# Paged attention with gathers of eight-key rows, five sets of pages, and the next weights loaded at the end of the stage

## What is computed

```
def paged_attend(q_lat, q_pe, ckv_new, kpe_new, cache_ckv, cache_kpe, page_table, layer):
    ...
    def page_step(carry, pages):
        ck = cache_ckv[layer, pages]
        kp = cache_kpe[layer, pages]
        return online_update(carry, mla_scores(q_lat, q_pe, ck, kp), ck), None
    carry, _ = lax.scan(page_step, init, page_table.T)
```

## Time and profile before

| | us |
|---|---|
| median of 3 runs | 3132.86 |
| lowest, highest | 3125.3, 3133.38 |
| the profiled execution: span from first to last instruction | 3130.1 |
| PE busy in it | 2904.4 (93%) |
| DVE busy | 1737.1 (55%) |
| POOL busy | 1274.1 (41%) |
| ACT busy | 1076.9 (34%) |
| `stage_paged` in it, first to last matmul of the stage (lines 3158 to 3222) | 601.8 to 1039.5 |

### The profile page before, as it was taken

One profiled execution on the slowest core, in us unless ns is written; L12 is line 12 of the kernel. 1 busy time (PEld: TensorE's weight loads), 2 busy tenths in 40 slices (PEclk: granted clock), 3 DMA queues, 4 the chain that ended last, 5 costly groups with the idle time before them and its releaser, 6 DMA issues. The chain is left out here.

```text
span 3130.1 us, 60385 instructions
## 1 busy us (share of the span) xinstructions
PE 2904.4 (93%) x24873; PEld 2612.3 (83%) x24873; DVE 1737.1 (55%) x3025; ACT 1076.9 (34%) x2174; POOL 1274.1 (41%) x899
## 2 busy tenths in 40 slices
PE   6999899898899898999999998898898999999996
PEld 4888576566656798999999997887898999999996
DVE  5331245465555477666665237787477666664234
ACT  5411136421111464333331015575464333331012
POOL 2411157633333463444443114686553444443112
PEclk8999989898888999999999999999999999999999
DMA  9455300255554241232237322311331223246322
GB/s 318 163 201 182 103 22 1 89 177 178 189 183 163 78 132 56 98 112 93 103 116 276 110 102 86 87 30 30 85 119 63 96 100 112 85 139 252 140 81 79
DMA packets 241598, 377.90 MB, mean 121 GB/s; under 512 B 15531, under 2 KB 156204, under 8 KB 241061
## 3 DMA queue, kind: packets, MB, share of 16 engines
q1 hardware_dynamic: 200092, 253.95, 24.6%
q0 software_dynamic: 20992, 75.51, 7.2%
q10 hardware_dynamic: 20240, 44.57, 3.9%
HBM read 298.71 MB, written 73.28 MB: 119 GB/s over the span
## 5 line engine op out<-in xcount | busy, mean ns | idle before, releaser
L791 PE MATMUL ps<-HS,w_split 128*128 128x272 f32 x1920 | 272.2, 292 | 23.9 <-ACT sg L1048 10.4
L791 PEld LDWEIGHTS ps<-HS,w_split 128*128 128x128 f32 x1920 | 252.7, 190 | 29.8 <-ACT sg L1048 15.5
L807 PE MATMUL ps<-HS,w_ring 128*128 128x272 f32 x1920 | 273.0, 288 | 0.0
L807 PEld LDWEIGHTS ps<-HS,w_ring 128*128 128x128 f32 x1920 | 253.8, 189 | 0.0
L2312 PEld LDWEIGHTS ps<-HS_in,w_split 128*128 128x128 f32 x1728 | 222.7, 191 | 27.7 <-issue 16.4
L2312 PE MATMUL ps<-HS_in,w_split 128*128 128x272 f32 x1728 | 233.6, 294 | 9.2 <-DVE HS_in L2531 9.1
L1786 DVE TENSOR_TENSOR Y<-Y,ps 128x272 f32<-128x272 f32 x256 | 111.9, 437 | 224.9 <-PE ps L807 224.9
L1384 POOL TENSOR_TENSOR w_split<-w_raw,w_split 128x512 fp32r<-128x512 f32 x120 | 169.6, 1427 | 156.8 <-ACT w_split L1040 156.8
L762 PE MATMUL ps<-HS,w_ring 128*128 128x272 f32 x1344 | 179.8, 295 | 18.1 <-PEq L156 12.1
L762 PEld LDWEIGHTS ps<-HS,w_ring 128*128 128x128 f32 x1344 | 175.7, 193 | 20.5 <-POOLq L1433 12.3
L1384 POOL TENSOR_TENSOR w_ring<-w_raw,w_ring 128x512 fp32r<-128x512 f32 x40 | 61.5, 1538 | 270.1 <-ACT w_ring L1040 270.1
(11 more groups left out here) (496 smaller groups left out, 6695.9 us busy)
## 6 DMA issues: line engine op xcount, KB each, us to landing
hid_spill<-hid SPq DMA_DIRECT2D x40, 1088.0 KB, 7.4
w_mod_half<-w_mod_in SPq DMA_DIRECT2D x40, 1024.0 KB
HS<-hid_spill ACTq DMA_DIRECT2D x32, 1088.0 KB, 11.8
w_raw<-w_ffn_gate_in SPq DMA_DIRECT2D x44, 512.0 KB
w_raw<-w_ffn_up_in SPq DMA_DIRECT2D x44, 512.0 KB, 6.0
w_raw<-w_ffn_down_in SPq DMA_DIRECT2D x44, 512.0 KB
x_part<-x_spill SPq DMA_DIRECT2D x54, 272.0 KB, 2.9
x_spill<-Y SPq DMA_DIRECT2D x12, 1088.0 KB, 5.5
```

The costliest lines, as they stand in the source:

```text
L791: ins = pe.matmul(psum(U.banks(u)[b]), part_slot(j, a)[:, k, :], token_part(n, j, e)[:, k, :], start=(j < 3 and k == 0 and i == 0), stop=( ...
L807: ins = pe.matmul(down_bank(n), slots[DOWN_SLOT[t]][:, a, d * P:(d + 1) * P], hid_cols(k, t, q)[:, e, :], start=(t == lo and j == 0), stop ...
```

## The change

1. **Rows of eight keys.** The row table counts rows of 8 keys (`ROWK`, `NROWK = 8`), so a `cache_ckv` gather brings 8 KB per partition, 1 MB in all, and there are two for a period, one for each sequence, where there were four.
2. **Five sets of pages.** The buffers are five sets (`NSETS`) of one period each: `w_raw` with one old slot (`first.units[0]`), two sets in `q_all`, a new tile `pages_ckv1`, and `pages_ckv2`, which lies over slots 2 and 3 of the weight ring. DVE waits once for a period's whole set.
3. **When gathers are issued.** The gathers of period h wait for `scored` to count h-2, which is the end of `scores(h-3)`, and for `values(h-5)`. The `cache_kpe` gathers of an even h come after its two `cache_ckv` gathers, not before them. In `stage_attention` the early gathers bring set 0 and the two at its end bring set 1.
4. **The next weights come at the end.** SP loads the two `w_out_ab` tiles after `values(30)`, ACT splits them after `copy_p(31)` and ahead of the last copy into `Y`, and POOL after its last gather.

```diff
     def gather_pages(...)
-        i, j = g // NG, g % NG
-        blocks = c.cache_ckv[0].rearrange("n (h k) r -> (n h) (k r)", h=2 * NG)
-        pool.indirect_dma_start(out.rearrange("p a r -> p (a r)"), None, blocks,
-                                bass.IndirectOffsetOnAxis(c.ckv_rows[:, 2 * i + e, j:j + 1], 0)).then_inc(done, 16)
+        i, n = h // NUNIT, NROWK // NUNIT
+        blocks = c.cache_ckv[0].rearrange("n (h k) r -> (n h) (k r)", h=2 * NROWK)
+        for s in range(n):
+            j = h % NUNIT * n + s
+            pool.indirect_dma_start(out[:, s * ROWK:(s + 1) * ROWK, :].rearrange("p j r -> p (j r)"), None, blocks,
+                                    bass.IndirectOffsetOnAxis(c.ckv_rows[:, 2 * i + e, j:j + 1], 0)).then_inc(done, 16)
 ...
     stage_paged, SP
-            sp.wait_ge(valued, 1)
-            for t in range(2):
-                sp.dma_start(ring[0][t][:, :].rearrange("p (k n) -> p k n", k=KD), w_cols(w_next, t * P)).then_inc(w_in[t], 16)
             rows(1)
             rows(2)
             rows(3)
             sp.wait_ge(scored, H)
             sp.dma_start(wkv, c.w_kv_up[0].rearrange("(k p) n -> p k n", p=P)).then_inc(wkv_in, 16)
+            sp.wait_ge(valued, 2 * (H - 2) + 2)
+            for t in range(2):
+                sp.dma_start(ring[0][t][:, :].rearrange("p (k n) -> p k n", k=KD), w_cols(w_next, t * P)).then_inc(w_in[t], 16)
 ...
     stage_paged, POOL
-            for g in range(4, G):
-                if g % 2 == 0 and (g - NPB - 3) // 2 in AHEAD:
-                    t = AHEAD.index((g - NPB - 3) // 2)
-                    pool.wait_ge(w_hi, t + 1)
-                    pool.tensor_tensor(ring[1][:, t, 1, :], ring[0][t][:, :], ring[1][:, t, 0, :].bitcast(F32), ALU.subtract
-                                       ).then_inc(w_lo, 1)
-                if g % (NG // NQK) == 0:
-                    v = g // (NG // NQK)
+            for h in range(2, H):
+                if h >= 3:
+                    pool.wait_ge(scored, h - 2)
+                if h >= NSETS:
+                    pool.wait_ge(valued, 2 * (h - NSETS) + 2)
+                for e in range(2):
+                    first.gather_pages(pool, c, units[h % NSETS][e], h, e, p_in[h % NSETS])
+                if h % 2 == 0:
+                    v = h // 2
                     if v >= 2:
                         pool.wait_ge(kturned, (v - 1) * (NG // NQK))
                     for e in range(2):
                         first.gather_kpe(pool, c, pk[v % 2][e], v, e, k_in[v % 2])
-                if g > NPB:
-                    pool.wait_ge(valued, g - NPB + 1)
-                for e in range(2):
-                    first.gather_pages(pool, c, page(g, e), g, e, p_in[(g - 1) % NPB])
+            for t in range(2):
+                pool.wait_ge(w_hi, t + 1)
+                pool.tensor_tensor(ring[1][:, t, 1, :], ring[0][t][:, :], ring[1][:, t, 0, :].bitcast(F32), ALU.subtract
+                                   ).then_inc(w_lo, 1)
 ...
     stage_paged, DVE, turn(g)
-                dve.wait_ge(p_in[(g - 1) % NPB], 32 * ((g - 1) // NPB) + 32)
+                if g % 2 == 0:
+                    h = g // 2
+                    dve.wait_ge(p_in[h % NSETS], PAGES_IN * (h // NSETS) + PAGES_IN)
```

More of the change, by code:

```diff
@@ L2131, in _ @@
             dve.tensor_copy(c.sta[:, :, :], c.ps[:, 1, 0:64].rearrange("p (k r) -> p k r", k=KA))
-            for n, per in ((0, 2 * NG), (1, 2 * NQK)):
+            for n, per in ((0, 2 * NROWK), (1, 2 * NQK)):
                 dve.tensor_scalar(page_row[:, n, :], c.ps[:, 1, P:P + NB], float(per), None, ALU.mult).then_inc(rows_set, 1)
@@ L2653, in __init__ @@
         nc = c.nc
-        self.pages = [c.raw_front[e][:, :].rearrange("p (j r) -> p j r", j=G4) for e in range(2)]
-        second = tile(nc, cm, "pages_ckv0", [P, 2, G4, KR])
+        n = 2 * G4 * KR
+        self.second = tile(nc, cm, "pages_ckv0", [P, 2 * G4, KR])
+        raw = nc.alloc_sbuf_tensor_at(f"pages_first_{nc.next_id()}", [P, 2 * G4, KR], F32, offset=c.raw_at)
         self.queries = tile(nc, cm, "q_all", [P, NH * T])
-        n = 2 * G4 * KR
-        self.slots = [second] + [self.queries[:, u * n:(u + 1) * n].rearrange("p (e j r) -> p e j r", e=2, j=G4) for u in range(4)]
+        self.units = [[raw[:, :, :], self.second[:, :, :]]]
+        self.units += [[self.queries[:, (2 * u + e) * n:(2 * u + e + 1) * n].rearrange("p (j r) -> p j r", r=KR) for e in range(2)]
+                       for u in range(2)]
         self.kpe = tile(nc, cm, "pages_kpe0", [P, 2, NG // NQK, G4 * ROPE])
@@ L2734, in stage_attention @@
         sc = [c.ps[:, 2 * u:2 * u + 2, :].rearrange("p a n -> p (a n)") for u in range(2)]
-        wkv_all = first.slots[0][:, :, :, :].rearrange("p k j r -> p k (j r)")
+        wkv_all = first.second[:, :, :].rearrange("p (k j) r -> p k (j r)", k=2)
         own = c.ps[:, 0, 0:NPAIR * NSA]
@@ L3033, in _ @@
             pool.wait_ge(k_made, NH // 2)
-            for e in range(2):
-                first.gather_pages(pool, c, first.slots[0][:, e, :, :], 1, e, first.slots_in[0])
+            first.gather_pages(pool, c, first.units[0][1], 0, 1, first.units_in[0])
             for u in range(NU):
@@ L3041, in _ @@
             pool.wait_ge(scored, NU)
-            for g in (2, 3):
-                for e in range(2):
-                    first.gather_pages(pool, c, first.slots[g - 1][:, e, :, :], g, e, first.slots_in[g - 1])
+            for e in range(2):
+                first.gather_pages(pool, c, first.units[1][e], 1, e, first.units_in[1])
 def stage_paged(c, ckv, ctok, qlat, qpe, yb, ring, w_next, first):
@@ L3060, in stage_paged @@
     with Stage(nc) as cm:
-        NPB = 7
-        slots = first.slots + [tile(nc, cm, f"pages_ckv{u}", [P, 2, G4, KR]) for u in range(len(first.slots), NPB)]
+        last = tile(nc, cm, "pages_ckv1", [P, 2, 2 * G4, KR])
+        spare = nc.alloc_sbuf_tensor_at(f"pages_ckv2_{nc.next_id()}", [P, 2, 2 * G4, KR], F32, offset=c.ring_at + 4 * 4 * KD * P)
+        units = first.units + [[t[:, e, :, :] for e in range(2)] for t in (last, spare)]
         pk = [[first.kpe[:, 0, :, :], first.kpe[:, 1, :, :]],
@@ L3074, in stage_paged @@
         mx = [tile(nc, cm, f"run{u}", [P, 5]) for u in range(2)]
-        AHEAD = (3, 4)
         w_in = sems(nc, cm, "w_in0", "w_in1")
         w_hi, w_lo = sems(nc, cm, "w_hi", "w_lo")
-        p_in = first.slots_in + sems(nc, cm, *[f"ckv_in{u}" for u in range(3, NPB)])
+        p_in = first.units_in + sems(nc, cm, *[f"ckv_in{u}" for u in range(2, NSETS)])
         k_in = [first.kpe_in] + sems(nc, cm, "kpe_in1")
@@ L3100, in page @@
         def page(g, e):
-            return first.pages[e] if g == 0 else slots[(g - 1) % NPB][:, e, :, :]
+            return units[g // 2 % NSETS][e][:, g % 2 * G4:g % 2 * G4 + G4, :]
         @block.sync
@@ L3253, in _ @@
                 copy_p(h)
-                if h in AHEAD:
-                    t = AHEAD.index(h)
-                    act.wait_ge(w_in[t], 16)
-                    act.activation(ring[1][:, t, 0, :], ring[0][t][:, :], ACT.Copy).then_inc(w_hi, 1)
+            for t in range(2):
+                act.wait_ge(w_in[t], 16)
+                act.activation(ring[1][:, t, 0, :], ring[0][t][:, :], ACT.Copy).then_inc(w_hi, 1)
             act.wait_ge(y_made, 1)
```

32 lines of the change are left out of this document (19 added, 13 removed).

## The result

On the chip of the first measurement the changed kernel takes 3053.5 us (median of 4 runs, 3049.6 to 3060.4) against 3133.1 us (3125.3 to 3133.9): a ratio of 0.976, 95% interval 0.974 to 0.978. That is 79.6 us less; the forecast was 121.5 us less. The profiled execution is the slowest of the four.

The account below looks back on a forecast made before the run. The prediction took PE to be starved of instructions while POOL issues gathers and 1 to 2 us after. -115 - 6 - 1 + 0.5 = -121.5 us, 3130.1 to 3008.6 profiled, 3011 median; own range 2997 to 3030, widened to 3058.

Parts of the forecast that it names:

- Periods without stops: Paged attention, periods 3 to 29: 8.9 us without cache_kpe gathers, 9.6 us with them, against 11.0 and 16.1 before.
- POOL's cost does not double: POOL's page gathers: 0.94 us each with eight-key rows; the rival of twice that gave 3045 us, chance 0.08.
- two rivals: Gathers costing POOL twice (3045 us, chance 0.08) and gather bytes starving PE (3058 us, chance 0.07); range widened to 2997-3058 us.
- 14 x 8.9 + 13 x 9.6: The 27 periods: 14 without cache_kpe gathers and 13 with them take 249.4 us against 366.3.
- The term of -115 us: The 27 periods: moving gathers to the end of the scores gains 117 us, less 2 us for query row loads.
- bytes in flight: Rival in the 27 periods: gather bytes, not their issue, starve PE; periods of 9.9 and 12.1 us, 3058 us, chance 0.07.
- First period: First period of paged attention: four gathers issued instead of ten release the matmuls sooner, -6 us, bounds -4 and -10.
- End of `stage_attention`: Before the barrier ending stage_attention: two gathers in place of four, same bytes, -1 us, bounds 0 and -3.
- Next weights at the end: End of the paged attention stage: loading and splitting the next weight tiles after values(30) costs +0.5 us, bounds 0 and +3.
- The cover that I named: End of the stage: its last work, ending at 1040.0, hides the second weight tile's split, done at 1039.5, by half a microsecond.
- The sign: Whole kernel: the change makes it faster by more than 0.3%, chance 0.95; same 0.02, slower 0.03.
- the 117 us: The 27 periods: gain from 366.3 to 249.4 us by ending PE's starvation while POOL issues gathers.

Follow-up runs that it names:

- the version with the early weights: spread with the two next weight tiles loaded two periods earlier, after values(28), and split after copy_p(30): 3018.5 us, against 3042.0 for the changed kernel beside it.
- spread: Changed kernel with each period's second page gather put off to the end of values(h-4), any cache_kpe gathers ahead of it: 3022.4 us, ratio 0.967 to the kernel before.

## Where the prediction was right and where not

- **Periods without stops: right.** 8.77 and 9.6 us against 8.9 and 9.6, gathers of 0.948 us for 8 KB rows (so POOL's cost does not double), first gather 4.3 us ahead of the scores, one break in the scores with `cache_kpe` and none without. DVE never waited long for a set.
- **The range.** 3053.5 us lies outside the forecast's own range of 2997 to 3030 us. It lies inside 2997 to 3058 only because that range was widened for two rivals, so the sum did not earn it.
- **The step that failed is in the sum 14 x 8.9 + 13 x 9.6**, the claim that every period would be undisturbed ("even 1.9 us later it is over", "no loss of clock is counted"). The term of -115 us measured 366.3 - 292.0 = -74.3. The missing 41 us are mostly 12 block stops (29.7 us) and the time at half clock that follows some (24 us in the 27 periods, which costs up to 12); four shorter stops of 0.9 to 1.3 us stand at such boundaries in `values` (h = 3, 14, 16 and 25). I had asked only what stops instructions while POOL issues. That a shorter period needs its blocks sooner, while the bytes now end later relative to the scores, is the question I did not ask. On the first kind the kernel before shows no such stop; the likely reason, which no run tests, is that starvation made its scores 6 to 12 us long, so that a block had longer to come.
- **The rival "bytes in flight"** had the mechanism (the block waits behind the gathers' bytes) and a chance of 0.07. Its price, 296 us for the 27 periods, is near the 292 measured, but it spread the loss over all periods and put it in place of the starvation by issue. The runs show both side by side: the second kind of chip has block stops alone, the first kind has both. So that the measured time is near this rival's is in part luck. The reason I gave against it, that breaks end with the issue, was true of the breaks that I looked at and said nothing on others.
- **First period: right**, the first maxes come 5.5 us sooner (-6), although PE starts the stage 1.2 us later. Not foreseen: period 1 is also 3.2 us shorter. **End of `stage_attention`**: PE starts 1.2 us later, not 1 sooner.
- **Next weights at the end: wrong in size.** +0.5 us was forecast, bounds 0 and +3; it is 3.0 us from the last maxes to the copies and 3.2 in the barrier, outside the bounds. I had looked at when the splits end (by 955.6 they are over, ahead of the copies), not at who works beside POOL. The cover that I named hid the splits' length but not their effect on DVE.
- In sum, to the start of the next stage: -8.7 to the end of h = 2, -74.3, and +6.2 at the end of the stage, -77 us; the profiled execution then lost 5 us over the rest of the program. It is the slowest of its four runs, and their median, 79.6 us less, shows no such loss.
- **The sign** was right for the chip predicted on and for one other. It does not hold on the second kind, where the starvation that the 117 us were to be won from is not there. No row of the first profile could have told this.

## What to carry over

Read a break in PE that waits for no semaphore by its place: if the distances between breaks are multiples of 256 instructions (its semaphore instructions counted too), it is most likely a block that came late, and the remedy that worked here is a gap in the bytes when the block is asked for, not fewer issues: with such a gap the 27 periods took 259.7 us in place of 292.0 on the first kind and, in the version with the early weights, 266.4 in place of 284.0 on the second. A gain that rests on such breaks should be measured on several chips before it is believed; here it was 2.4% on one kind and a loss of 0.5% on the other. `spread` with the early weights is the version to keep: 3018 us on the second kind, better than both there; on the first kind `spread` alone gave 3022, and the two together weren't run on it.

## What was not expected of the hardware

- Chips differ in this. With the same program, six gathers issued across the scores cost 7.3 us a period on two chips and nothing on two others, with POOL's rows (0.94 us), the DMA time (200 us) and the program behind the stage (2089 and 2091 us) alike. One chip of the second kind showed the short time twice, twenty minutes apart; whether a chip can change its kind is open. What in the chip differs is open, and so is whether on the first kind it is the issue itself or the bytes just behind it that starves PE; the runs there moved the two together.
- One 16 KB instruction packet started only after 1.1 to 2.6 MB of gather bytes had moved on another queue since the boundary before it. The Trainium skill ("DMA: Bandwidth & Descriptors", Arbitration) has each DMA engine change between queues packet by packet, with some 9 to 17 descriptors in a packet. If a row of 8 KB (309 ns in the profile) is a whole packet, the block would have waited 0.3 us, and the trace disagrees; if it is one descriptor, the wait would be 2.8 to 5.3 us, which is of the size seen. Both are estimates, and no run here tells which holds. In the twelve stops the packet started 3.0 to 8.0 us behind the boundary before, in place of 1.1 to 1.4, and 4 KB rows left stops of up to 2.5 us.
